# A 13-phase fp32 transformer kernel: the high weights of the 256-token phases go through both activation parts in one 512-column matmul

## The reference, cut to what matters

```python
def swiglu(x, w_gate, w_up, w_down):
    return (jax.nn.silu(x @ w_gate) * (x @ w_up)) @ w_down
# first block (272 tokens: 16 meta + 256), 2 layers
h = h + 0.5 * swiglu(rmsnorm(h, ffn1_norm[l]), ...)      # 1024 -> 2816 -> 1024
h = h + hybrid_mixer(rmsnorm(h, mix_norm[l]), ...)       # attention, convolution, gates
h = h + 0.5 * swiglu(rmsnorm(h, ffn2_norm[l]), ...)
# final norm, the meta tokens are dropped
# second block (256 tokens), 2 layers
h = x + 0.5 * _swiglu(_rms(x, ffn1_norm[i]), ...)
h = h + (differential attention | retention)(_rms(h, mix_norm[i]))
x = h + 0.5 * _swiglu(_rms(h, ffn2_norm[i]), ...)
```

## Time and profile before

| | |
|---|---|
| time, median of 2 runs | 2198.81 us (2191.77 to 2205.85) |
| the profiled execution's own time | 2198.7 us |
| its span, first to last instruction | 2196.9 us |
| TensorE busy | 2185.1 us, 18114 matmuls |
| VectorE / ScalarE / GpSimd busy | 1602.3 / 1277.0 / 282.8 us |

### The profile page before, as it was taken

How to read it: one execution, slowest core, us unless ns; L and a number is a source line. 1 busy time by engine, 2 the same in 40 slices (tenths; PEclk the granted TensorE clock), 3 DMA queues, 4 the chain that set the end, 5 groups by cost and what they waited for, 6 DMA issues and landing times.

```text
span 2196.9 us, 48980 instructions
## 1 busy us (share of the span) xinstructions
PE 2185.1 (99%) x18114; PEld 2167.6 (99%) x18114; DVE 1602.3 (73%) x2450; ACT 1277.0 (58%) x1988; POOL 282.8 (13%) x328
## 2 busy tenths in 40 slices
PE   8999999999999999999999999999999999999999
PEld 8999999999999999999999999999999999999999
DVE  6655998665566579887768767988778766777775
ACT  6444886544444369766556646876556545565652
POOL 0001652000100145220020011010010010101000
PEclk9999999999999999999999999999999999999999
DMA  6555435555455444455545555355655655446563
GB/s 233 179 193 164 161 124 170 170 179 190 157 178 192 166 169 136 157 188 184 196 156 201 197 176 167 116 188 194 200 180 195 210 165 184 154 163 200 183 201 124
DMA packets 100408, 386.68 MB, mean 176 GB/s; under 512 B 11312, under 2 KB 12464, under 8 KB 100304
## 3 DMA queue, kind: packets, MB, share of 16 engines
q1 hardware_dynamic: 99648, 383.89, 52.4%
q0 software_dynamic: 368, 1.26, 0.2%
q10 hardware_dynamic: 288, 0.12, 0.0%
HBM read 384.18 MB, written 1.05 MB: 175 GB/s over the span
## 4 chain that ended last, share of the span: by engine, by line
PE 96%; DVE 2%; ACT 1%; issue 0%; DMA 0%; SPq 0%; ACTq 0%
PE bank L399 15%; PE bank L401 15%; PE bank L400 15%; PE bank L407 15%; PE bank L408 15%; PE bank L409 15%; PE bank L771 1%; PE bank L1061 1%; PE bank L1062 1%; PE bank L1063 1%; DVE wlo L424 1%; PE bank L1108 0%; PE bank L721 0%; PE bank L752 0%; PE bank L952 0%; PE bank L955 0%
## 5 line engine op out<-in xcount | busy, mean ns | idle before, releaser
L424 DVE TENSOR_TENSOR wlo<-raw,whi 128x1024 fp32r<-128x1024 f32 (+1 forms) x677 | 893.8, 1322 | 178.2 <-ACT whi L417 165.9
L417 ACT ACTIVATE whi<-raw 128x1024 fp32r<-128x1024 f32 (+1 forms) x677 | 745.6, 1112 | 154.7 <-PE bank L401 107.6
L399 PE MATMUL bank<-u,whi 128*128 128x272 f32 (+1 forms) x1888 | 546.5, 289 | 7.4 <-DVE u L462 7.1
L401 PE MATMUL bank<-u,wlo 128*128 128x272 f32 (+1 forms) x1888 | 541.1, 287 | 0.0
L400 PE MATMUL bank<-u,whi 128*128 128x272 f32 (+1 forms) x1888 | 535.9, 284 | 0.0
L407 PE MATMUL bank<-u,whi 128*128 128x256 f32 x1888 | 528.7, 280 | 0.2
L408 PE MATMUL bank<-u,whi 128*128 128x256 f32 x1888 | 526.9, 279 | 0.0
L409 PE MATMUL bank<-u,wlo 128*128 128x256 f32 x1888 | 526.9, 279 | 0.0
L399 PEld LDWEIGHTS bank<-u,whi 128*128 128x128 f32 x1888 | 355.7, 188 | 8.5 <-DVE wlo L424 7.8
L409 PEld LDWEIGHTS bank<-u,wlo 128*128 128x128 f32 x1888 | 357.4, 189 | 0.0
L407 PEld LDWEIGHTS bank<-u,whi 128*128 128x128 f32 x1888 | 356.4, 189 | 1.0 <-DVE wlo L424 0.5
(11 more groups left out here) (332 smaller groups left out, 3448.7 us busy)
## 6 DMA issues: line engine op xcount, KB each, us to landing
raw<-w SPq DMA_DIRECT2D x552, 512.0 KB, 3.4
raw<-w SPq DMA_DIRECT2D x128, 704.0 KB, 4.2
h<-xT SPq DMA_DIRECT2D x4, 272.0 KB, 5.3
outT<-h SPq DMA_DIRECT2D x8, 128.0 KB, 4.7
consts<-cst POOLq DMA_DIRECT2D x1, 576.0 KB, 4.8
dist<-cst POOLq DMA_DIRECT2D x1, 192.0 KB, 3.4
rdist<-cst POOLq DMA_DIRECT2D x1, 192.0 KB, 3.7
sgain<-small POOLq DMA_DIRECT2D x1, 145.5 KB, 5.4
```

The costliest lines, as they stand in the source:

```text
L399: pe.matmul(out, w_h, x_hi, start=first, stop=False)
L401: return pe.matmul(out, w_l, x_hi, start=False, stop=last)
L417: act.activation(weights(0, n), raw[:, n % RING, 0:COLS[n]].rearrange("p (k c) -> p k c", c=128), ACT.Copy).then_inc(hi_ready, 1)
L424: dve.tensor_tensor(weights(1, n), raw[:, n % RING, 0:COLS[n]].rearrange("p (k c) -> p k c", c=128), weights(0, n), ALU.subtract).then_inc ...
```

## The change

The two matmuls with the high weights, L407 and L408, become one of 512 columns. For that the high and the low part of a tile lie side by side: in u and hid from phase 5 on (tile_of), and in ry. Beside that, the first tile (k = 0) of each gate and up panel has its 512-column matmul cut in two at a column that the table CUTS gives for the phase and the panel's place j in the ring; a cut at 0 is none. Each piece is a matmul with a weight load of its own.

```diff
+CUTS = {5: (0, 256, 128, 384), 7: (64, 448, 192, 320), 9: (508, 500, 496, 480), 10: (16, 32, 240, 272),
+        12: (252, 244, 260, 504)}
...
-            ry = sb("ry", [128, 2, 16, SEQ], f32r, area)
-            ry_hi, ry_lo = ry[:, 0, :, :], ry[:, 1, :, :]
+            ry = sb("ry", [128, 16, 2, SEQ], f32r, area)
+            ry_hi, ry_lo = ry[:, :, 0, :], ry[:, :, 1, :]
...
+            if y > LAST_MIX:
+
+                parts = buf[:, place[0]:place[0] + tiles * 2 * SEQ].rearrange("p (k c) -> p k c", c=2 * SEQ)
+                return parts[:, k, part * SEQ + c0 - first:part * SEQ + c1 - first]
...
+        def both_of(buf, place, tiles, k):
+            return buf[:, place[0]:place[0] + tiles * 2 * SEQ].rearrange("p (k c) -> p k c", c=2 * SEQ)[:, k, :]
...
-        def split_products(pe, out, n, k, x_hi, x_lo, first, last):
+        def in_two(pe, out, w, x, cut, first):
+
+            cols = x.shape[-1]
+            if cut:
+                pe.matmul(out[:, 0:cut], w, x[:, 0:cut], start=first, stop=False, skip_group_check=True)
+                first = False
+            pe.matmul(out[:, cut:cols], w, x[:, cut:cols], start=first, stop=False, skip_group_check=True)
+
+        def joined_products(pe, out, n, k, x, first, last, cut=0):
...
-            pe.matmul(out[:, 0:SEQ], w_h, x_hi, start=first, stop=False, skip_group_check=True)
-            pe.matmul(out[:, SEQ:2 * SEQ], w_h, x_lo, start=False, stop=last, skip_group_check=True)
-            return pe.matmul(out[:, 0:SEQ], w_l, x_hi, start=False, stop=last, skip_group_check=True)
+            in_two(pe, out, w_h, x, cut, first)
+            return pe.matmul(out[:, 0:SEQ], w_l, x[:, 0:SEQ], start=False, stop=last, skip_group_check=True)
...
-                                mm = split_products(pe, bank[g % 4], n, k, u_at(uy, 0, k),
-                                                 u_at(uy, 1, k), k == 0, k == KD - 1)
+                                mm = joined_products(pe, bank[g % 4], n, k, both_of(u, U_PLACE[uy], KD, k),
+                                                     k == 0, k == KD - 1, CUTS[y][j] if k == 0 else 0)
```

More of the change, by code:

```diff
@@ L659, in ffn, with out_proj, tile @@
                 out_proj(y, b["P"] + 2 * FT, 2, HALF, lambda part, k: hid_at(y, part, k),
+                         lambda k: both_of(hid, HID_PLACE[y], FT, k),
                          hid_ready, b["F"] + FT, N)
-            def out_proj(y, n0, per_tile, tiles, x, ready, count, N, lag=3):
+            def out_proj(y, n0, per_tile, tiles, x, both, ready, count, N, lag=3):
                 group, joined = RING // per_tile, N == SEQ
-                def tile(j, it, both):
+                def tile(j, it, wide):
                     pe.wait_ge(h_done, KD * (y + 1) + j - 1 + group * it)
@@ L675, in tile @@
                                 pe.wait_ge(ready, count - (lag if K == 0 else last - K))
-                            if both:
-                                mm = split_products(pe, bank[4 + j % 2], n, k, x(0, K), x(1, K), K == 0, K == last)
+                            if wide:
+                                mm = joined_products(pe, bank[4 + j % 2], n, k, both(K), K == 0, K == last)
                             else:
@@ L863, in in_panel2 @@
                     if PHASES[y] == "rt" and acc < 4 * RT_HEADS:
-                        mm = split_products(pe, bank[panel_bank(acc)], b["P"] + j, k, u_at(y, 0, k), u_at(y, 1, k),
+                        mm = joined_products(pe, bank[panel_bank(acc)], b["P"] + j, k, both_of(u, U_PLACE[y], KD, k),
                                              k == 0, k == KD - 1)
@@ L1118, in rt @@
                                       stop=True).then_inc(r_osum, 1)
-                out_proj(y, b["P"] + 48, 2, KD, lambda part, k: ry[:, part, k, :], r_y_ready,
+                out_proj(y, b["P"] + 48, 2, KD, lambda part, k: ry[:, k, part, :],
+                         lambda k: ry[:, k, :, :].rearrange("p a c -> p (a c)"), r_y_ready,
                          16, SEQ, lag=6)
```

## The result

The changed kernel takes 2222.57 us (2222.23 and 2222.91), the kernel before 2198.81 (2191.77 and 2205.85): a ratio of 1.0129 with a 95% interval from 1.0081 to 1.0176, slower by 1.3%. The forecast was 2206.

The account below looks back on a forecast made before the run. TensorE was taken as the bound, by matmul count times start distance. Joined work went from 965.1 to 960.6 us, plus 11.5 for cuts: +7.0 on 2198.7, forecast 2206 us, range 2178 to 2225.

Parts of the forecast that it names:

- What bounds the kernel, and the two gaits: TensorE throughout: time is matmul count times start distance; a tile's three matmuls steadily take 353.3 or 339.9 ns.
- What is a pair worth: Feed-forward phases: one 512-column plus one 256-column matmul takes 346.8 ns; 2770 of them gain 4.5 us.
- its own last paragraph: Test in a 256-token phase: forecast wrong if the 512 + 256 distance is none of 346.8, 342.5, 351.0, 333, 327 ns.
- Slow gait all through: Joined stream: every 512 + 256 columns take 351.0 ns, loss 7.2 us plus 11.5 for cuts, 2217 us; chance 0.2.
- The fee for each matmul: Joined stream: time above a column a clock, 6.6 or 11.0 ns, is paid once per matmul; 2184 us, chance 0.12.
- a column a clock: Joined stream: 512 activation columns go at one per clock, 326.6 ns with the 256-column matmul; 2150 us, chance 0.06.
- What the cuts add: Gate and up panel heads: 209 extra matmuls, each piece costing the larger of 111 ns and 0.4515 per column; 11.5 us.
- What costs nothing: Other engines' writes at new places and TensorE's waits add no term; VectorE stays below the bound.
- The sum: Whole kernel: 965.1 becomes 960.6 + 11.5 = 972.1 us, +7.0; with the surrounding 1.8 us, 2206 us.

Follow-up runs that it names:

- ten cuts: Kernel before, with the first matmul of panels three and four cut at columns 4 and 252 in each 256-token phase's first round: 2179.71 us, ratio 0.9935.
- the split stream of 256 columns: Kernel before, with the first 256-column matmul of gate and up panels cut in two at 16 different columns, some panels uncut: 2202.58 us, ratio 1.0031.

## Why the prediction was wrong, by its steps

- **What bounds the kernel, and the two gaits** (353.3 and 339.9 ns, a whole phase at a time, drawn at interruptions): right, and shown by ten cuts that turn every phase fast. What I missed is that the two runs hid how the times are spread: by its time, the kernel before has in most executions (17 of 28) one fast phase more than the profiled one and takes 2192 us.
- **What is a pair worth**: this step failed. I built a pair of 512 + 256 columns from rows of 512 alone and of 256 alone, 342.5 to 351.0 ns, and took the middle, 346.8. It is 353.3, above both ends. The sentence "so I expect both gaits to occur and take the middle" is the wrong one: a gait belongs to the sequence of widths, not to each matmul, and this sequence is back in its slow one from the sixth pair of a panel at the latest, even where a cut had just given it 113 and 226 ns. Instead of a gain of 4.5 us it is a loss of 13.6. By its own last paragraph the forecast is wrong, since 353.3 is none of the distances named there.
- **Slow gait all through** was the nearest rival: 2217, with 0.2. It had the pair at 351.0; with 353.3 it gives 2198.7 + 13.6 + 11.5 = 2224. By its own 344.3 ns from which the change loses, the result's sign was decided by that one number. That 2222.57 still lies in the range is luck: its upper end has this rival's 2217 and 7 us for unchanged phases in another gait, and those kept their gaits; it was the pair that cost more.
- **The fee for each matmul, a column a clock**: both wrong. A third of the weight loads went, and a slow triple and the pair take the same 353.3 ns. The prediction took N / 2.4 + 2.5 ns from the Trainium skill, page "TensorE: Matmul & The Clock Gate", section "Back-to-back issue gap", as if it were meant for such a stream. That section gives it for a single matmul by itself, and for streams with a weight load at each matmul it gives about 131 ns at 512 columns. Neither agrees with this case, where 512 columns took 229 to 235 ns (215.8 by the rule).
- **What the cuts add**: near in mechanism, mis-sized by 1.5 us. Where looked at closely the price at the cut fits: 0.33 us for 16 + 496 columns (335 ns priced), 107.5 ns for each cut at 508 (109 priced). Per round and phase 11.5 us had been 106, 213, 415, 206, 108 ns; by the rates above (a pair less 353.3, times 32) they were 74, 163, 387, 182, 83. The fast pairs behind a cut, in the changed kernel, gave back most of the difference: loop panels cut at 192 and 320 cost 0 and 7 ns beside eight pairs of 353.3, not 24 each. One went the other way, 448, at 93 for 82 priced, and in the split stream of 256 columns a cut cost 113 to 140, so the rule for a piece is a rough one.
- **What costs nothing**: right. The new places cost nothing (1.0013 [0.9989, 1.0036]), and TensorE stayed the chain.
- **The sum**: 2198.7 + 13.6 + 10.0 = 2222.3 beside 2222.57.

## What to carry to other kernels

Where TensorE is busy all the time, read the distance between starts of equal matmuls phase by phase: if one stream has two steady distances, the first thing to win is the better one for all of it, and a single odd matmul ahead of a loop can bring it (here 0.6% for ten matmuls of some 100 ns). Cheaper on paper, fewer and wider matmuls, can leave only the worse one; try the new sequence of widths by itself before building on it. And a group of times in equal steps from run to run tells of such states before any trace does.

## What the runs showed of the hardware

With a 128x128 fp32 weight load at each matmul and the clock at its full level all along, the steady distances of the feed-forward phases were 113.3 or 117.8 ns for 256 columns, 124.3 or 123.3 for 272 (gate and up, down), 233.3 for 512 and 353.3 for 512 + 256 (one only); 512 columns of moving weights went at 229 or 233.3. That is some 0.443 to 0.460 ns a column, whatever the number of loads. These values are not all: in phase 8, whose projections go through products, 256 columns went at 116 and 118.4 ns in the kernel before (8.0 / 23 / 3 and 20.6 / 58 / 3), and no run tells why.

```profile
L400 PE MATMUL bank<-u,whi x24: 274/274/278, 899.8 to 907.8; 128*128 128x256 f32 x24
L400 PE MATMUL bank<-qk,whi x59: 281/281/283, 932.1 to 952.7; 128*128 128x256 f32 x59
```

A 256-column stream of a feed-forward phase keeps its distance for over 1500 matmuls, through loop turns and panel changes, and an odd matmul of as little as 4 columns can switch it, to the same side in every round of a loop. In the kernel before, 128x128 weight loads start no closer than 0.108 us to each other, but for three of 17857 distances. From that and 0.4515 ns a column I estimate that a piece of fewer than some 245 columns costs about 111 ns, partly at the row behind it (a piece of 4 columns, then 203 ns instead of 118).
